# A streaming encoder layer on one core: the first chunk of its second stage spread among projection rounds, and block products, masks and stores put in another place of a hand-written order

## What is computed

```python
h = rms_norm(x, norm_pre)
p = jnp.einsum('btd,dc->btc', h, w_in).astype(f32)
...
prev = jnp.concatenate([s_shift.astype(f32)[:, None], p_shift[:, :-1]], axis=1)
xm = p_shift + rwkv_mu.astype(f32) * (prev - p_shift)
r, kr, vr, wd, ad = jnp.split(...)
w = jnp.exp(-RWKV_DECAY_SCALE * jax.nn.sigmoid(rwkv_w0 + jnp.tanh(wd) @ rwkv_w_up))
a = jax.nn.sigmoid(rwkv_a0 + ad @ rwkv_a_up)
kk = kr * rwkv_k_k
kr = kr * (1.0 + (a - 1.0) * rwkv_k_a)
kk = kk / jnp.maximum(jnp.sqrt(jnp.sum(kk * kk, -1, keepdims=True)), 1e-12)
# per token:
#   s = s * w + (s @ -kk) (kk * a) + v k ;  y = s @ r
y, s_rwkv_new = rwkv7_recurrence(r, w, kr, vr, kk, a, s_rwkv)
...
o_rwkv = (groupnorm(y) + bonus) * jax.nn.silu(z_r)
m = jnp.einsum('btc,cd->btd', concatenate([o_gla, o_rwkv]), w_out)
x = x + rms_norm(m, norm_post)
```

## Time and profile before

| | |
|---|---|
| median of three runs | 2319.01 us (2316.41 to 2319.48) |
| profiled execution: time, span | 2315.25 us, 2313.5 us |
[...]
| TensorE busy | 2242.2 us, 97% |
| VectorE, ScalarE, GpSimd busy | 63%, 56%, 25% |
| second stage | from 923 us; bodies 1 to 14 from about 1055 to 1931 us, some 62 us each |

### The profile page before, as it was taken

How to read it: one execution, slowest core, us unless ns; L and a number is a source line. 1 busy time by engine, 2 the same in 40 slices (tenths; PEclk the granted TensorE clock), 3 DMA queues, 4 the chain that set the end, 5 groups by cost and what they waited for, 6 DMA issues and landing times. The chain is left out here.

```text
span 2313.5 us, 72365 instructions
## 1 busy us (share of the span) xinstructions
PE 2242.2 (97%) x31109; PEld 1704.8 (74%) x31109; DVE 1448.1 (63%) x2699; ACT 1284.4 (56%) x2757; POOL 578.2 (25%) x1070
## 2 busy tenths in 40 slices
PE   7999999999999998889999999999999998899998
PEld 5777777777777776777888888888888886544443
DVE  6444545444455554567777777777777777456675
ACT  8355555555555544645666666666666664343333
POOL 0000000000000000355555555555566565000000
PEclk9999999999999999999999999999999999999999
DMA  6212222222333331222222333232223234666675
GB/s 245 69 56 70 80 79 89 79 79 90 105 108 117 101 101 50 52 59 70 72 72 78 83 87 87 78 81 67 72 82 87 84 88 141 204 213 214 223 237 182
DMA packets 217278, 244.62 MB, mean 106 GB/s; under 512 B 110080, under 2 KB 159552, under 8 KB 212608
## 3 DMA queue, kind: packets, MB, share of 16 engines
...
## 5 line engine op out<-in xcount | busy, mean ns | idle before, releaser
L2111 PE MATMUL first<-h,w_hi 128*128 128x256 f16 (+1 forms) x2496 | 419.1, 272 | 0.0
L2070 POOL TENSOR_TENSOR r_inv_tmp<-r_inv 64x30 f32<-64x30 f32 (+14 forms) x480 | 265.8, 554 | 412.8 <-DMA r_inv<-scratch_blocks 376.5
L748 PE MATMUL d<-h,w_hi 128*128 128x256 f16 (+1 forms) x2176 | 351.6, 270 | 0.0
L2111 PE MATMUL first<-h,w_lo 128*128 128x256 f16 (+1 forms) x1248 | 337.8, 272 | 0.0
L748 PE MATMUL d<-h,w_lo 128*128 128x256 f16 (+1 forms) x1088 | 290.6, 270 | 0.0
L2072 POOL TENSOR_TENSOR r_inv<-r_inv,r_inv_tmp 64x30 f32<-64x30 f32 (+14 forms) x480 | 279.7, 583 | 37.6
L2111 PEld LDWEIGHTS first<-h,w_hi 128*128 128x128 f16 x2496 | 237.6, 98 | 50.4 <-issue 18.9
L748 PEld LDWEIGHTS d<-h,w_hi 128*128 128x128 f16 x2176 | 209.5, 98 | 33.6 <-issue 3.9
L2013 POOL MEMSET r_run_s<- 128x128 f16 x1 | 0.2, 204 | 917.9 <-POOLq L390 917.9
L748 PE MATMUL first<-h,w_hi 128*128 128x256 f16 (+1 forms) x1168 | 184.5, 268 | 5.0 <-DVE w_lo L1236 3.1
L2111 PE MATMUL r_d<-h,w_hi 128*128 128x256 f16 (+1 forms) x960 | 158.8, 271 | 0.8 <-DVE carry_s L2742 0.8
...
## 6 DMA issues: line engine op xcount, KB each, us to landing
...
```

The costliest lines, as they stand in the source:

```text
L748: mm = pe.matmul(out, lhs(k, a, w), rhs(k, a, w), start=(n == 0), stop=(n == len(terms) - 1))
L2070: step(pool.tensor_tensor(tmp, inv[0:n, 0:u, u:u + 1].to_broadcast([n, u, w]), inv[0:n, u:u + 1, u + 1:32].to_broadcast([n, u, w]), ALU.mult))
L2111: mm = pe.matmul(out, lhs(k, a, w), rhs(k, a, w), start=(m == 0), stop=(m == 3 * KT - 1))
```

## The change

Four edits, all to the order in which instructions stand; none is added or taken away but one wait.

1. **Opening.** Chunk 0's jobs, which stood in a row behind all rounds of block 1, are spread: `scores` behind round x6, `inner` and `turn` behind the second piece of x10, `solve` and `join` behind the fourth. On VectorE `masked` comes behind `mixed:x6`, `td` and `keep_w` behind `strict`, ahead of `mixed:x8`.
2. **Block products.** x8's pieces stood as two, `meet`, `scores`, four, `inner`, `unknowns`, `turn`, `xs`. Now: four, `meet`, `scores`, `xs`, two, `inner`, `unknowns`, `turn`. In the bodies without rounds the same places hold output units.
3. **VectorE and ScalarE.** `clamp:1` is directly behind `clamp:0`; `k_prime` ahead of `next:2`; `low:0` behind `join_o:3`; `beta` and `a` ahead of `td`, `masked:4`, `zc:3`; `strict` ahead of `mixed:x8`. On ScalarE `high:0` is behind both `rnorm`.
4. **SP.** `put_m:0` is behind `inverse_back`.

The ring keeps its order; a second numbering, `FULL_NO`, follows the order in which rounds are finished, since `xs` is now full before x8, and the waits on full banks use it. `mixed` of block 2's x12 gets a wait for `kappa` of block 1 on its own engine.

```diff
@@ tables
-    x8*2 meet:3 scores:4 out x8*4 inner:4 unknowns:3 turn:4 xs variance:1 out x10*2 advance:3 solve:4 join:4
+    x8*4 meet:3 scores:4 xs out x8*2 inner:4 unknowns:3 turn:4 variance:1 out x10*2 advance:3 solve:4 join:4
...
-    -td masked:4 zc:3 beta a mixed:x8 strict:0 out strict:1 even:3 keep_w:4 normed:1 rkk next:3 join_o:4 gated:1
+    -td masked:4 zc:3 strict:0 out strict:1 mixed:x8 even:3 keep_w:4 normed:1 rkk next:3 join_o:4 gated:1
...
-    -put_m:1 out -bonus_out out out out out get_gate:0 out put_m:0 -inverse_back out out blocks_out blocks_in
+    -put_m:1 out -bonus_out out out out out get_gate:0 out -inverse_back out out put_m:0 blocks_out blocks_in
...
+FIRST_CHUNK = {("x6", 6): ("scores",), ("x10", 2): ("inner", "turn"), ("x10", 4): ("solve", "join"),
+               ("mixed", "x6"): ("masked",), ("strict", "1"): ("td", "keep_w")}
+
 def opening_jobs(table):
...
+                for job in script_jobs(name, arg, b, int(n or 1)):
+                    yield job
+                    pieces[name] = pieces.get(name, 0) + 1
+                    if b == 1:
+                        for first in FIRST_CHUNK.get((name, pieces[name] if name in XROUNDS else arg), ()):
+                            yield first, 0
...
+FULL_NO = {key: n for n, key in enumerate(full_order())}
...
                 if m >= NBANK:
                     released(ROUND_KEYS[m - NBANK])
-                return bank_of(key), m
+                return bank_of(key), FULL_NO[key]
...
             for n, jobs in enumerate(PE_JOBS):
                 run(jobs, does)
-                if n == 0:
-                    scores(0)
-                    inner(0)
-                    turn(0)
-                    solve_ahead(0)
-                    join_inverse(0)
...
+                if r == "x12" and b == 2:
+                    dve.wait_ge(kap_ok.sem, kap_ok.at(b - 1, 1))
```

More of the change, by code:

```diff
@@ L1326 @@
     out tanh:la0 squares:0 tanh:lw2 tanh:la2 deviation:0 odd:1 out turned:2 k_factor taken:x6 z1:2 keep_y:1
-    join_e:2 affine:0 squares:2 out gamma taken:x0 odd:2 turned:3 high:0 rnorm:0 out rnorm:1 z1:3 join_e:3
+    join_e:2 affine:0 squares:2 out gamma taken:x0 odd:2 turned:3 rnorm:0 out rnorm:1 high:0 z1:3 join_e:3
     keep_y:2 taken:x2 centred:1 out taken:x8 odd:3 turned:4 out deviation:1 affine:1 z1:4 join_e:4 keep_y:3
@@ L1333 @@
     out masked:2 zc:1 decay out even:1 keep_w:2 normed:0 next:1 mixed:x6 join_o:2 gated:0 out masked:3 zc:2
-    clamp:0 even:2 mixed:x0 keep_w:3 clamp:1 low:0 out unit:0 unit:1 next:2 join_o:3 k_prime mixed:x2 out
-    -td masked:4 zc:3 beta a mixed:x8 strict:0 out strict:1 even:3 keep_w:4 normed:1 rkk next:3 join_o:4 gated:1
+    clamp:0 clamp:1 even:2 mixed:x0 keep_w:3 out unit:0 unit:1 k_prime next:2 join_o:3 low:0 mixed:x2 beta out a
+    -td masked:4 zc:3 strict:0 out strict:1 mixed:x8 even:3 keep_w:4 normed:1 rkk next:3 join_o:4 gated:1
     kappa out
@@ L1339 @@
 SP_BODY = """
-    -put_m:1 out -bonus_out out out out get_gate:0 out put_m:0 -inverse_back out out blocks_out blocks_in
+    -put_m:1 out -bonus_out out out out get_gate:0 out -inverse_back out out put_m:0 blocks_out blocks_in
     get_gate:1 out
@@ L1420, in opening_jobs @@
                 name, _, arg = token.partition(":")
-                if name not in STEP + AHEAD + POST + ("out", "td"):
-                    yield from script_jobs(name, arg, b, int(n or 1))
+                if name in STEP + AHEAD + POST + ("out", "td"):
+                    continue
+                for job in script_jobs(name, arg, b, int(n or 1)):
[4 more added lines that the diff above has]
+                            yield first, 0
 OUT_UNITS = [(tile, n) for tile in range(SINGLES) for n in range(12)]
@@ L1552, with full_order @@
 ROUND_KEYS = list(ROUND_NO)
+def full_order():
+    ends = {}
+    for n, (job, arg) in enumerate(j for jobs in PE_JOBS for j in jobs):
+        if job == "piece":
+            ends[arg[:2]] = n
+        elif job == "out":
+            ends["out", arg[0], arg[1] // 6] = n
+        elif job in ("xs", "kn", "bs"):
+            ends.update({(arg, job + str(k)): n for k in range(2)})
+        elif job == "rank":
+            ends.update({(arg[0], r % arg[1]): n for r in ("lw%d", "la%d")})
+        elif job == "centre":
+            ends.update({(job, arg, k): n for k in range(2)})
+        elif job == "variance":
+            ends[job, arg] = n
+    return sorted(ROUND_KEYS, key=ends.get)
+FULL_NO = {key: n for n, key in enumerate(full_order())}
 AT = {}
@@ L1558 @@
 EARLY = ("x12", "x4", "x6")
-assert [ROUND_NO[0, r] for r in EARLY] == [0, 1, 2]
+assert [ROUND_NO[0, r] for r in EARLY] == [FULL_NO[0, r] for r in EARLY] == [0, 1, 2]
 def rwkv_phase(nc, t, c):
@@ L1893, in get_ow @@
                 if j == 0:
-                    m = ROUND_NO[LAST - 1, "x10"]
+                    m = FULL_NO[LAST - 1, "x10"]
                     sp.wait_ge(d_full.sem, d_full.at(m, 1))
@@ L1901, in get_npost @@
             def get_npost():
-                m = ROUND_NO[LAST, "x10"]
+                m = FULL_NO[LAST, "x10"]
                 sp.wait_ge(d_full.sem, d_full.at(m, 1))
@@ L2119, in piece @@
                 n = tiles(b) * P
-                out, m = bank_of((b, r)), ROUND_NO[b, r]
+                out, m = bank_of((b, r)), FULL_NO[b, r]
                 if h == 0 and third == 0:
@@ L2361, in project_out @@
                 h, sixth = n // 6, n % 6
-                m = ROUND_NO["out", tile, h]
+                m = FULL_NO["out", tile, h]
                 out = bank_of(("out", tile, h))
@@ L2666, in out_squares @@
                 tile, h = arg
-                act.wait_ge(d_full.sem, d_full.at(ROUND_NO["out", tile, h], 1))
+                act.wait_ge(d_full.sem, d_full.at(FULL_NO["out", tile, h], 1))
                 if tile:
```

28 lines of the change are left out of this document (13 added, 15 removed).

## The result

The changed kernel takes 2341.7 us (median of four runs, 2338.09 to 2344.21) against 2318.4 before (median of four, the three of the table above and one more): 1.0100 of it, 95% interval 1.0083 to 1.0118. It is 23.3 us slower; 7.1 were forecast, and the time lies outside the range of 2314 to 2332. The profiled execution has a span of 2336.3 us (time 2338.09), 22.8 more than before, at a mean granted TensorE clock of 0.990 (0.991 before).

What follows compares the result with a forecast made beforehand. TensorE, busy 97% of the span, was taken to bound the kernel. Terms -1.4 + 7.2 - 2.8 + 5.3 - 1.2 = +7.1 on 2315.25 gave 2322.4 us, 2326 on the median's scale; range 2314 to 2332.

Steps and rivals of the forecast that it cites:

- x10's bank: Blocks 3 to 15: x10 waits about 0.55 us for the bank x8 filled, in 13 bodies, +7.2 us.
- `xs`'s own wait: Middle bodies: `xs` no longer waits, as `a` is ready before `scores` ends; -1.4 us.
- Opening: Chunk 0 and blocks 0 to 2: 5.3 us of waits and half clock leave, 2.5 come; -2.8 us.
- R2: Rival: `xs` of block 0 waits 3 us or more, the clock falls, the opening gains nothing; some 2329; chance 0.11.
- 0.4 for shifts: Opening, block 2: allowance of 0.4 us for shifts, within the +2.5 of new waits.
- Block 16: Body 14: three waits leave, new waits of 1.6 at `xs` and 4.3 at x10, 1.5 of clock; +5.3 us.
- Store of m: Body 15: the inverse's way out no longer stands behind the store of m in SP's queue; -1.2 us.
- m itself is only needed later: SP's store of m: claim made beside the -1.2 us for placing it behind the inverse's way out.
- R1: Rival: x10's bank comes free in time, the middle costs nothing, block 16 keeps only 1.6; 2313; chance 0.15.
- R4: Rival: waits at x10 half as long, 0.3 each, block 16 at its lower end, +3.5; 2321; chance 0.14.
- R3: Rival: each new wait at x10 brings back half clock, 1.5 us each in 13 bodies; 2346; chance 0.03.
- Slower: Whole kernel: measured time above 2323.6 us; chance 0.66.

Runs made afterwards that it cites:

- the kernel with the longer release: Changed kernel with `low:0` and `high:0` back, plus `rkk`, `even:3`, `keep_w:4` put ahead of `mixed:x8` on VectorE: ratio 1.0089 to the kernel before.

## Where the prediction was right and where it failed

**x10's bank.** Right in mechanism, place and size. The release comes 2.78 us after x8 (2.85 said). TensorE would arrive 2.21 after x8 (2.29 said): 1.25 to `variance`, and from there 0.96 where x10 doesn't wait. So each body stands 0.57 longer where 0.55 was put; that both ends were 0.07 to 0.08 off in the same direction is luck, but a small one. In thirteen bodies the step from `variance` to x10 grew by 6.5 where 7.2 was put, since in two of them a stall elsewhere had used up the release.

**`xs`'s own wait.** Here the prediction failed. The step is the sentence that `a` is ready before `scores` ends, with its term -1.4. It looked at what had moved ahead of `a` and never at what `low:0` releases: `r_yT`, which ScalarE's `odd:2` writes, with `taken:x2` behind it. The change's own text named the move of `low:0`. Counted from one start to the next, the matmuls of `xs` and the steps into and out of its old and new places take 6.7 us more in thirteen bodies: the term is +6.7 and not -1.4. With `low:0` back the same count is -2.3: the wait cost 8.9, and the early place of `xs` alone wins a little, as was said. Block 16's wait grew too. The bodies as a whole became 7.8 shorter with `low:0` back: shown.

**The rest of the bodies.** The other +3.8 are mostly stalls inside rows of equal matmuls (idle 0.95, 1.39, 0.53, 1.07, where before there was one of 0.73). Counted from start to start they make the head sums `bs` (L2179 before, the line of `kn` too) 4.7 us longer in all; everything else is 0.9 shorter. Nothing in the prediction spoke of these stalls. The new order of the bodies isn't needed for them: in the kernel with the spread opening alone they are as long (4.7).

**Opening.** Removed as said: the waits at chunk 0 and the half clock behind them are gone. But the first `meet` comes only 2.0 us earlier, counted from the second stage's first projection matmul, and all of it is gone by chunk 4: +0.1 instead of -2.8. `xs` of block 0 waits 2.94 (3.0 to 3.3 said) and block 1's 1.22 (1.1 said). Two things were missed. The clock falls behind the 2.94, 1.7 us. That is R2's mechanism, given 0.11, and R2's "the opening gains nothing" came true; but its condition, a wait of about 3 us, is not what decides, since the clock fell behind 2.41 in other profiles as well. And in body 0 `k_prime` ahead of `next` makes the advance wait 1.86, with 1.5 of clock behind it, where the prediction had "0.4 for shifts"; with `next:2` ahead again that wait is gone. With the opening alone the gain is eaten by the inverse of block 1, a chain that the prediction didn't look at; `inner` of chunk 2 waited 0.94 before, too.

**Block 16.** The walk along `turn`, `turned`, `ow_high`, `ow_low`, `strict`, `mixed` gave 4.3; measured 4.22. The term is +7.6 instead of +5.3 because `xs` waited 2.9 (1.3 more than said, 0.8 of it `low:0`'s by the experiment) and 2.9 us went at half clock (1.5 said); the old waits that left are 2.4 (2.1 said, where the earlier trace rows have 0.8 in two at `inner` and the prediction took only the longer). The experiment with the split moved shows the mechanism, and that block 16 was not the last word: bodies 15 and 16 gave most of the gain back.

**Store of m.** -1.2 was wrong. SP, body 15, before and after:

```profile
1977.65 1.24 SPq L1843 DMA_DIRECT2D scratch_mr<-r_m_hl  x1
1978.93 0.49 SPq L1871 DMA_DIRECT2D scratch_inverse<-r_inv  x1
...
1996.14 2.04 SPq L1965 DMA_DIRECT2D w_hi<-scratch_tw  x1
1998.22 1.52 SPq L1966 DMA_DIRECT2D w_lo<-scratch_tw  x1
1999.79 1.55 SPq L1904 DMA_DIRECT2D scratch_inverse<-r_inv  x1
```

The store's 1.24 us did leave, but the way out of the inverse now took 1.55 to issue instead of 0.49. Whichever instruction came first behind the two loads took over a microsecond, and from the loads' end to the inverse's it is 1.77 before and 1.55 after: 0.2 won. The wait at `inner` of chunk 62 went from 3.67 to 3.59. "m itself is only needed later" overlooked the other side: not who reads m, but who writes the next m into its buffer.

**The rivals.** R1 and R4 named too small a loss, R3 the right size (2346) with a cause that isn't there: over waits of 0.40 and 0.47 in every body the granted clock of 1060 to 1905 us is 1.00, and so it is over those of 1.09 in the kernel with the longer release. Two pauses of some 0.4 us in each body of about 63 us brought no fall here. R4 also took +3.5 as block 16's lower end, where its own section says +2.

**The chances.** Slower had 0.66 and was right. The range ended at 2332 because every bound in it was a bound of a term that I had found; nothing stood for a wait of some tenths per body that I had not found, and thirteen bodies multiply that, nor for stretches at half clock that come in one execution and not in the next.
